# Attention and decode sampling in a decoder layer: an earlier place for the modulation pieces, far keys in their place, one load queue, and another order at the end of mixing

## The chip, the cores and the metric

The kernel runs on one core of a Trainium2 chip. A core has five engines, each with its own instruction stream: TensorE (PE in the profile, its weight loads PEld), VectorE (DVE), ScalarE (ACT), GpSimd (POOL) and SyncE (SP). They wait for one another through semaphores. Transfers are issued by an engine onto its queue (SPq, ACTq, POOLq) and are carried by DMA engines; the profile counts sixteen of them. The metric is the device time of one execution in microseconds; lower is better.

## The reference, cut to what matters

One step of one layer for a prompt of 1024 tokens and for eight decode sequences ("samples") of four new tokens each, with a cache of 2048 keys and values per sequence.

```
mod = silu(c) @ w_ada + b_ada;  sh1, sc1, gt1, sh2, sc2, gt2 = split(mod)
u = x * (1 + sc1) + sh1;  xa, ga, q, k, v = split(u @ w_in)
y_a = rglru_branch(xa, ga)                      # recurrent branch
y_b = merge over (window, dilation) in (128,1), (512,4), (2048,16) of softmax(q k^T / 8) v
      # sample: keys = cache of 2048 rows and the 4 new ones
mixed = concat(rms_norm(y_a), rms_norm(y_b)) @ w_out
x1 = layer_norm(alpha * x + gt1 * mixed);  u2 = x1 * (1 + sc2) + sh2
out = layer_norm(alpha * x1 + gt2 * hier_moe(u2))   # 4 groups x 4 experts, top 2
also returned: the caches with the new rows appended (k_win_sample, v_win_sample, ...)
```

A sample's query needs the last 512 rows of the cache (near) and, of the 1536 rows before, four of every sixteen (far).

## The kernel before

The program is a row of stages, each a block of five instruction streams that ends with a barrier: `front` (input projection, recurrent branch, part of the modulation), `attention` (prompt), `sampling` (the eight sequences), `mixing` (output projection, first layer norm, router logits), `routing`, `experts`, `finish`. Every order is written out by hand; nothing is scheduled by a planner.

**attention** goes through 32 steps, 4 pairs of heads times 8 query tiles of 128. Step `s` has `t = s % 8` and attends to `t + 1` key blocks, so a round of eight steps grows from short to long. In a step TensorE makes the scores of step `s + 2`, turns the probabilities of `s`, and multiplies the values of `s - 1`; VectorE masks and takes maxima, ScalarE makes exponentials. Beside this, `modulate(n)` (L1126 to L1132) computes one of 16 pieces of the modulation that the first stage left over: two groups (halves of the remaining columns) of eight row blocks, four matmuls of 512 columns each that add into one accumulator `psM`. It sits in odd steps: `if s % 2 == 1: modulate(s // 2)`. The weights of a piece (1 MiB) come through a ring of four, `a_wring`, which SP fills again once the piece four back is done (`s_mm`). VectorE adds the bias to a finished group at steps 15 and 31 and so frees the accumulator (`s_me`). After each fourth ring load SP issues a copy of one sequence's value cache, 4 MB from memory to memory (`out_v_s`); behind the ring it loads the near keys of the first four sequences into `ring0`, then the new rows. SP ends the stage with a wait for the copies.

**sampling** works on two groups of four sequences. Cached keys and values come as 32 pieces through ten slots: key pieces 0 to 15 (near and far of the first group, then of the second), value pieces 16 to 31 in the same order. A near piece is 512 rows (1 MiB); a far piece is 96 strips of four rows (0.75 MiB). Slots 0 to 3 are `ring0`, the others `ring1` (`s_ring` in the profile). SP loads near pieces (`near_load`), ScalarE far pieces (`far_load`, L1541 to L1545, at seven places of its stream). A load into a used slot waits for `consumed(n - 10)`, a count of transposes (`s_tp`) or of value units (`s_pv`). Sixteen units `u` turn the keys: 0 to 3 near and 4 to 7 far of the first group, 8 to 15 the second. `turn(u, h)` transposes, ScalarE and VectorE evict one half each, `scores(u)` multiplies. `squares` (L1491 to L1497) sums the squares of the attention output for its norm: ScalarE makes four chunks of 1024 columns, TensorE adds them, two token tiles in each of units 4 to 7. `values(g, part)` multiplies near (part 0) and far (part 1) values. At the end SP loads half of the output weights into the room of slots 2 and 3 (`wo_early`).

**mixing** takes eight token tiles of 128 and one tile of the 32 sample rows (`t = 8`): `product`, `residual`, `deviation`, `normalize`, `modulate` (giving `u2`), then router logits by way of `turn_u`, `turned_u`, `router`, `partial`, `gather`, `route`. POOL makes `x1` from the normalized tile, SP stores `x1` and then `u2` of a tile, and at the end waits until all have landed. The tail after the last product serves tiles 6, 7 and 8.

## Time and profile before

| | us |
|---|---|
| three runs | 1475.36, 1482.18, 1482.31 (median 1482.18) |
| profiled execution | 1476.67, its span 1474.9 |
| attention | 346.9 to 506.3 |
| sampling | 506.3 to 638.7 |
| mixing | 638.7 to 777.0 |
| routing, experts, finish | 777.0 to the end |

A stage begins in the table where SP issues its first load. Over the span TensorE is busy 1233.1 us (84%), VectorE 732.4 (50%), ScalarE 580.6 (39%), POOL 155.0 (11%); the mean granted clock of TensorE is 0.907. SP's queue (q1) carries 260 MB of the 316 MB, ScalarE's (q10) 32 MB. The shares are means over stages with different limits, so they are read stage by stage. In a timeline an instruction's line ends with the idle time of its engine just before it and what ended that. For a tile, the profile lists its transfers with the time from issue to landing (least, median, most).

### The profile page before, as it was taken

The page shows a single profiled execution, that of the slowest core. Times are in us where ns is not written, and L with a number is a line of the kernel's source. Part 1 is how long each engine was busy: PE and PEld are TensorE (multiplying, and loading weights), DVE is VectorE, ACT ScalarE, POOL GpSimd, SP SyncE. Part 2 cuts the span into 40 slices and gives each one's busy share as a digit, 9 for nine tenths or more (in the row PEclk, how much of TensorE's full clock was granted, in tenths as well). Part 3 has the DMA queues.
Part 4 walks back from the last instruction along what each step waited for, and adds up shares of the span by engine and source line. Part 5 has one row for each costly group of instructions (what it writes and reads, how often), then busy time and mean ns, then how long its engine had stood idle before and what let it go on. Part 6 is the DMA issues. An engine that isn't in the chain of part 4 may idle for free. (4 is left out here: it accounts for less than half of the span.)

```text
span 1474.9 us, 21260 instructions
## 1 busy us (share of the span) xinstructions
PE 1233.1 (84%) x7040; PEld 939.7 (64%) x7041; DVE 732.4 (50%) x1238; ACT 580.6 (39%) x849; POOL 155.0 (11%) x146
## 2 busy tenths in 40 slices
PE   5799899997999778589960389999999999989762
PEld 3799777783555567158740267777778878778520
DVE  3357515434666425255533365788531454673147
ACT  3554532102555413133320354677421453662123
POOL 0000000000000000004333300011000000000064
PEclk8899999997999968789975599999999999999976
DMA  9967811298866457964313385999541666573193
GB/s 337 353 237 273 292 68 60 95 338 300 307 235 237 132 158 235 277 207 149 118 60 124 133 292 203 364 365 362 209 179 57 228 228 227 206 263 115 50 379 130
DMA packets 103278, 316.42 MB, mean 215 GB/s; under 512 B 14157, under 2 KB 23037, under 8 KB 96538
## 3 DMA queue, kind: packets, MB, share of 16 engines
q1 hardware_dynamic: 83738, 260.30, 50.0%
q10 hardware_dynamic: 12464, 31.87, 6.7%
q0 software_dynamic: 7008, 23.34, 4.7%
q8 instruction: 42, 0.69, 0.2%
q14 instruction: 26, 0.21, 0.0%
HBM read 281.17 MB, written 101.43 MB: 259 GB/s over the span
## 5 line engine op out<-in xcount | busy, mean ns | idle before, releaser
L2597 PE MATMUL e_psY<-e_downh,e_hTh 128*128 128x512 f32 x224 | 96.2, 429 | 27.9 <-DVE e_hTl L2553 27.9
L2532 DVE TENSOR_TENSOR e_downl<-e_wd,e_downh 128x1024 fp32r<-128x1024 f32 x64 | 74.1, 1219 | 76.7 <-ACT e_downh L2432 76.7
L2599 PE MATMUL e_psY<-e_downl,e_hTh 128*128 128x512 f32 x224 | 91.1, 407 | 0.0
L2597 PE MATMUL e_psG<-e_gateh,e_xTh 128*128 128x512 f32 x224 | 90.8, 405 | 0.2
L2598 PE MATMUL e_psY<-e_downh,e_hTl 128*128 128x512 f32 x224 | 91.0, 406 | 0.0
L2597 PE MATMUL e_psG<-e_uph,e_xTh 128*128 128x512 f32 x224 | 90.8, 405 | 0.0
L2598 PE MATMUL e_psG<-e_gateh,e_xTl 128*128 128x512 f32 x224 | 90.5, 404 | 0.0
L2599 PE MATMUL e_psG<-e_gatel,e_xTh 128*128 128x512 f32 x224 | 90.2, 403 | 0.0
L2598 PE MATMUL e_psG<-e_uph,e_xTl 128*128 128x512 f32 x224 | 88.6, 395 | 0.0
L2599 PE MATMUL e_psG<-e_upl,e_xTh 128*128 128x512 f32 x224 | 88.6, 395 | 0.0
L546 PE MATMUL n_psA<-n_wh,u_h 128*128 128x512 f32 (+1 forms) x216 | 88.0, 407 | 0.4 <-DVE n_wl L805 0.4
L548 PE MATMUL n_psA<-n_wh,u_l 128*128 128x512 f32 (+1 forms) x216 | 85.9, 397 | 0.0
L547 PE MATMUL n_psA<-n_wl,u_h 128*128 128x512 f32 (+1 forms) x216 | 85.6, 396 | 0.0
L2437 ACT CAST e_xTh<-e_psT 128x512 fp32r<-128x512 f32 x56 | 32.7, 584 | 130.8 <-PE e_psT L2592 130.8
L2425 ACT CAST e_gateh<-e_wg 128x1024 fp32r<-128x1024 f32 x64 | 62.3, 1045 | 52.3 <-POOLq L2495 39.7
L2432 ACT CAST e_downh<-e_wd 128x1024 fp32r<-128x1024 f32 x64 | 62.4, 1046 | 49.9 <-DMA e_wd<-in_w_exp_down 25.0
L2526 DVE TENSOR_TENSOR e_gatel<-e_wg,e_gateh 128x1024 fp32r<-128x1024 f32 x64 | 74.1, 1220 | 13.0 <-ACT e_gateh L2425 12.9
L2526 DVE TENSOR_TENSOR e_upl<-e_wu,e_uph 128x1024 fp32r<-128x1024 f32 x64 | 74.0, 1217 | 3.6 <-ACT e_uph L2425 3.6
L2597 PEld LDWEIGHTS e_psY<-e_downh,e_hTh 128*128 128x128 f32 x224 | 43.7, 195 | 38.9 <-issue 30.7
L2425 ACT CAST e_uph<-e_wu 128x1024 fp32r<-128x1024 f32 x64 | 62.4, 1049 | 5.9 <-issue 4.5
L2537 DVE TENSOR_TENSOR e_xTl<-e_psT,e_xTh 128x512 fp32r<-128x512 f32 x56 | 38.5, 687 | 49.1 <-ACT e_xTh L2437 49.0
L2502 POOL COPY e_ids<-ids 128x1 int32 (+1 forms) x28 | 12.1, 431 | 436.3 <-PE e_psT L2592 436.3
(391 smaller groups left out, 2661.7 us busy)
## 6 DMA issues: line engine op xcount, KB each, us to landing
e_wg<-in_w_exp_gate SPq DMA_DIRECT2D x16, 2048.0 KB
e_wu<-in_w_exp_up SPq DMA_DIRECT2D x16, 2048.0 KB
e_wd<-in_w_exp_down SPq DMA_DIRECT2D x16, 2048.0 KB, 10.7
out_k_s<-in_cache_win_k SPq DMA_DIRECT2D x8, 4088.0 KB, 21.5
out_v_s<-in_cache_win_v SPq DMA_DIRECT2D x8, 4088.0 KB, 33.7
a_wring<-in_w_ada SPq DMA_DIRECT2D x16, 1024.0 KB, 7.7
scratch_y<-e_y ACTq DMA_DIRECT2D x56, 256.0 KB, 6.7
n_wr<-in_w_in SPq DMA_DIRECT2D x20, 512.0 KB, 7.4
```

Of the source, the lines that this page charges most:

```text
L546: nc.tensor.matmul(dst, lh, rh, start=(k == 0), stop=False)
L547: nc.tensor.matmul(dst, lh, rl, start=False, stop=False)
L548: last = nc.tensor.matmul(dst, ll, rh, start=False, stop=(k == KD - 1))
L2425: nc.scalar.copy(w[name][H_][:, k:k + 2, :], ew[name][:, k:k + 2, :]).then_inc(s_wh.sem, s_wh.unit)
L2432: nc.scalar.copy(w["down"][H_][:, k, :], ew["down"][:, k, :]).then_inc(s_dh.sem, s_dh.unit)
L2437: nc.scalar.copy(xT[H_][:, par, 4 * half:4 * half + 4, :], psT[:, :, :]).then_inc(s_xh.sem, s_xh.unit)
L2526: nc.vector.tensor_tensor(w[name][L_][:, 2 * i:2 * i + 2, :], ew[name][:, 2 * i:2 * i + 2, :], w[name][H_][:, 2 * i:2 * i + 2, :], ALU.sub ...
L2532: nc.vector.tensor_tensor(w["down"][L_][:, k, :], ew["down"][:, k, :], w["down"][H_][:, k, :], ALU.subtract).then_inc(s_dl.sem, s_dl.unit)
L2537: nc.vector.tensor_tensor(xT[L_][:, par, blocks, :], psT[:, :, :], xT[H_][:, par, blocks, :], ALU.subtract).then_inc(s_tc.sem, s_tc.unit)
L2597: nc.tensor.matmul(dst, left[H_], right[H_], start=first, stop=False)
L2598: nc.tensor.matmul(dst, left[L_], right[H_], start=False, stop=False)
L2599: return nc.tensor.matmul(dst, left[H_], right[L_], start=False, stop=last)
```

## The change

**Attention.** `modulate(s - 1)` stands in each of steps 1 to 16; VectorE adds the bias at steps 8 and 16. The ring of weights lies in the room of four further slots, `ring0["far"]`. SP issues the 16 ring loads without copies between, then the near keys of the first group, two copies, then (once all pieces are done) the first group's far keys into that room, two more copies, and the new rows.

In attention SP's stream holds, from the third weight load on, before (`a_wring` are weights, `out_v_s` a cache copy, `ring` near keys):
```order
L1060 DMA a_wring<-in_w_ada 128x2048 x2
L1067 DMA out_v_s<-in_cache_win_v 64x16352
L1060 DMA a_wring<-in_w_ada 128x2048 x4
L1067 DMA out_v_s<-in_cache_win_v 64x16352
L1060 DMA a_wring<-in_w_ada 128x2048 x4
L1067 DMA out_v_s<-in_cache_win_v 64x16352
L1060 DMA a_wring<-in_w_ada 128x2048 x4
L1067 DMA out_v_s<-in_cache_win_v 64x16352
L1070 DMA ring<-in_cache_win_k 128x2048 x4
L1072 DMA out_k_s<-scratch_k_new 8x2048
```
and of the change (`ring_far` are far keys):
```order
L1067 DMA a_wring<-in_w_ada 128x2048 x14
L1074 DMA ring<-in_cache_win_k 128x2048 x4
L1059 DMA out_v_s<-in_cache_win_v 64x16352 x2
L1080 DMA ring_far<-in_cache_win_k 96x2048 x4
L1059 DMA out_v_s<-in_cache_win_v 64x16352 x2
L1084 DMA out_k_s<-scratch_k_new 8x2048
```
The four copies moved behind the weights, and four loads of far keys came in among them.

**Sampling.** Slots 0 to 3 are `ring0`, 4 to 7 `ring_far`, and two are left in `ring1`. All remaining pieces, 8 to 31, are loaded by SP in the order of their numbers; ScalarE loads none. The squares' four chunks are added into one by VectorE (`add_squares`, units 2 to 4), and TensorE sums that one for all tiles in unit 6, eight matmuls. `scale` of the recurrent branch comes one unit later.

In sampling ScalarE's stream, which evicts the turned keys (`s_kTs`), held these rows before, from its start to the first load that it issues between evictions:
```order
L1545 DMA s_ring<-in_cache_win_k 96x2048 x4
L1549 COPY s_kown<-kT 128x128
L1531 COPY s_kTs<-s_psK 128x1024
L1556 ACTIVATE s_sqb<-ybT 128x1024
...
L1531 COPY s_kTs<-s_psK 128x8x96 x4
L1539 CAST yah<-gelu_in 128x1024
L1531 COPY s_kTs<-s_psK 128x1024
L1545 DMA ring<-in_cache_win_k 96x2048 x2
L1545 DMA s_ring<-in_cache_win_k 96x2048 x2
```
and SP's stream of the change, from the second group's keys to the output weights:
```order
L1384 DMA s_ring<-in_cache_win_k 128x2048 x2
L1384 DMA ring<-in_cache_win_k 128x2048 x2
L1386 DMA ring<-in_cache_win_k 96x2048 x2
L1386 DMA ring_far<-in_cache_win_k 96x2048 x2
L1384 DMA ring_far<-in_cache_win_v 128x2048 x2
L1394 DMA s_bias<-in_k_sbias 128x928
L1384 DMA s_ring<-in_cache_win_v 128x2048 x2
L1386 DMA ring<-in_cache_win_v 96x2048 x4
L1384 DMA ring_far<-in_cache_win_v 128x2048 x4
L1386 DMA s_ring<-in_cache_win_v 96x2048 x2
L1386 DMA ring<-in_cache_win_v 96x2048 x2
L1400 DMA wo_early<-in_w_out 128x1024 x4
```
The loads of far pieces (96 rows) left ScalarE's stream and stand in SP's, between the near ones (128 rows).

**Mixing.** SP stores `u2` of a tile before `x1`. At the end TensorE turns tile 7 before it gathers tile 6; ScalarE takes the partial sums of tile 6, the turned tile 7 and then the sample tile's deviation, with tile 7's partial sums before the normalization; VectorE takes the logits of tile 6 ahead of the sample tile's `u2`, and makes the sample tile's `x1`, which POOL made before. The wait for the stores stands in POOL's stream of `experts`, ahead of its first fetch; their semaphores live outside the stage.

On VectorE the last rows of mixing were, from the sample tile's residual (`x_z`) on:
```order
L1919 TENSOR_TENSOR x_z<-x_psA,xs_gt 32x1024
...
L1949 TENSOR_TENSOR logits<-x_psR,x_br 128x20
L1929 RECIPROCAL x_col<-x_col 32x1
L1932 TENSOR_TENSOR x_col<-x_col 32x1
L1941 TENSOR_TENSOR x_u_6288<-x_z,xs_sc 32x1024
L1942 TENSOR_TENSOR x_u_6288<-x_u_6288,xs_sh 32x1024
L1949 TENSOR_TENSOR logits<-x_psR,x_br 128x20 x2
L1949 TENSOR_TENSOR logits<-x_psR,x_br 32x20
```
and are now:
```order
L1931 TENSOR_TENSOR x_z<-x_psA,xs_gt 32x1024
...
L1941 RECIPROCAL x_col<-x_col 32x1
L1944 TENSOR_TENSOR x_col<-x_col 32x1
L1961 TENSOR_TENSOR logits<-x_psR,x_br 128x20
L1953 TENSOR_TENSOR x_u_6267<-x_z,xs_sc 32x1024
L1954 TENSOR_TENSOR x_u_6267<-x_u_6267,xs_sh 32x1024
L1990 TENSOR_TENSOR x_x_6273<-x_z,x_lng 32x1024
L1992 TENSOR_TENSOR x_x_6273<-x_x_6273,x_lnb 32x1024
L1961 TENSOR_TENSOR logits<-x_psR,x_br 128x20
L1961 TENSOR_TENSOR logits<-x_psR,x_br 32x20
```
One row of logits moved ahead of the sample tile's `u2`, and two operations for `x1` came in behind it.

The diff, without the lines that only hand on semaphores and buffers:

```diff
-                if n % 4 == 3:
-                    sp.dma_start(ov[b:b + 1, 0:PAST - TS, :], cv[b:b + 1, TS:PAST, :]).then_inc(s_cp.sem, s_cp.unit)
+            copy(CT)
+            copy(CT + 1)
+            sp.wait_ge(s_mm.sem, s_mm.at(PIECES))
+            for c in range(4):
+                sp.dma_start(ring0["far"][0:FARM, c, :, :], rows.rearrange("(m i) n -> m i n", i=16)[:, 0:4, :]).then_inc(s_ring0[4 + c].sem, s_ring0[4 + c].unit)
+            copy(CT + 2)
+            copy(CT + 3)
...
-                if s % 2 == 1:
-                    modulate(s // 2)
+                if 1 <= s <= PIECES:
+                    modulate(s - 1)
...
-                if s % 16 == 15:
-                    g = s // 16
+                if s in (KD, PIECES):
+                    g = s // KD - 1
...
+        early = (ring0["slots"], ring0["far"], ring1)
+        slot = lambda n: early[n % RING // 4][:, n % RING % 4, :, :]
...
+            def load(n):
                 if n >= RING:
                     s, value = consumed(n - RING)
                     sp.wait_ge(s.sem, s.at(value))
-                sp.dma_start(slot(n), rows_of(n)[PAST - NEAR:PAST, :].rearrange("(p i) n -> p i n", i=4)).then_inc(s_ring[n % RING].sem, s_ring[n % RING].unit)
-            for n in (*range(8, 12), *range(16, 20), *range(24, 28)):
-                if n == 10:
+                if n // 4 % 2 == 0:
+                    sp.dma_start(slot(n), rows_of(n)[PAST - NEAR:PAST, :].rearrange("(p i) n -> p i n", i=4)).then_inc(s_ring[n % RING].sem, s_ring[n % RING].unit)
+                else:
+                    sp.dma_start(slot(n)[0:FARM], rows_of(n)[0:PAST - NEAR, :].rearrange("(m i) n -> m i n", i=16)[:, 0:4, :]).then_inc(s_ring[n % RING].sem, s_ring[n % RING].unit)
+            for n in range(8, PIECES):
+                if n == 8:
...
+            def squares():
+                pe.wait_ge(s_sq2.sem, s_sq2.at(3))
-                for t in (t, t + 1):
-                    for c in range(CT):
-                        last = nc.tensor.matmul(psS[:, 1, SQ + t:SQ + t + 1], sq[:, c, t * P:(t + 1) * P], ones[:, 0:1], start=(c == 0), stop=(c == CT - 1))
+                for t in range(NT):
+                    last = nc.tensor.matmul(psS[:, 1, SQ + t:SQ + t + 1], sq[:, 0, t * P:(t + 1) * P], ones[:, 0:1], start=True, stop=True)
                 last.then_inc(s_sqs.sem, s_sqs.unit)
-                if 4 <= u < KT_:
-                    squares(2 * (u - 4))
+                if u == 6:
+                    squares()
...
-                if u == KT_:
-                    for n in range(12, 16):
-                        far_load(n)
-                if u < CT:
-                    nc.scalar.activation(sq[:, u, :], ybT[:, u, 0:SEQ], ACT.Square).then_inc(s_sq.sem, s_sq.unit)
+                if u < CT // 2:
+                    for c in (2 * u, 2 * u + 1):
+                        nc.scalar.activation(sq[:, c, :], ybT[:, c, 0:SEQ], ACT.Square).then_inc(s_sq.sem, s_sq.unit)
...
+            def add_squares(i):
+                if i < 2:
+                    v.wait_ge(s_sq.sem, s_sq.at(2 * i + 2))
+                    c, d = 2 * i, 2 * i + 1
+                else:
+                    v.wait_ge(s_sq2.sem, s_sq2.at(2))
+                    c, d = 0, 2
+                nc.vector.tensor_tensor(sq[:, c, :], sq[:, c, :], sq[:, d, :], ALU.add).then_inc(s_sq2.sem, s_sq2.unit)
-                if 4 <= u < 4 + CT:
-                    scale(0, u - 4, first)
+                if 2 <= u <= 4:
+                    add_squares(u - 2)
+                if 5 <= u < 5 + CT:
+                    scale(0, u - 5, first)
...
-                sp.wait_ge(s_x1.sem, s_x1.at(t + 1))
-                sp.dma_start(dram["x1"][t * P:t * P + n, :], x1[0:n, t % 2, :]).then_inc(s_o1[t % 2].sem, s_o1[t % 2].unit)
                 sp.wait_ge(s_u2.sem, s_u2.at(t + 1))
                 sp.dma_start(dram["u2"][t * P:t * P + n, :], u2[0:n, t % 2, :]).then_inc(s_o2[t % 2].sem, s_o2[t % 2].unit)
+                if t < NT:
+                    sp.wait_ge(s_x1.sem, s_x1.at(t + 1))
+                else:
+                    sp.wait_ge(s_x1q.sem, s_x1q.at(1))
+                sp.dma_start(dram["x1"][t * P:t * P + n, :], x1[0:n, t % 2, :]).then_inc(s_o1[t % 2].sem, s_o1[t % 2].unit)
...
-            for s in (s_o1, s_o2):
-                sp.wait_ge(s[0].sem, s[0].at(NT // 2 + 1))
-                sp.wait_ge(s[1].sem, s[1].at(NT // 2))
...
-            for t in range(NTT):
-                n, par = rows_of(t), t % 2
+            for t in range(NT):
+                n, par = P, t % 2
...
+                if t == NT:
+                    route(t - 2)
...
-            route(NT - 2)
+            v.wait_ge(s_o1[0].sem, s_o1[0].at(NT // 2))
+            nc.vector.tensor_tensor(x1[0:NS, 0, :], z[0:NS, 0, :], lng[0:NS, :], ALU.mult).then_inc(s_gq.sem, s_gq.unit)
+            v.wait_ge(s_gq.sem, s_gq.at(1))
+            nc.vector.tensor_tensor(x1[0:NS, 0, :], x1[0:NS, 0, :], lnb[0:NS, :], ALU.add).then_inc(s_x1q.sem, s_x1q.unit)
             route(NT - 1)
             route(NT)
...
                 if t == NT:
+                    partial(t - 2)
                     turned_u(t - 1)
                 deviation(t)
+                if t == NT:
+                    partial(t - 1)
...
-                if t >= 1:
+                if 1 <= t < NT - 1:
                     partial(t - 1)
...
+            turn_u(NT - 1)
             gather(NT - 2)
-            turn_u(NT - 1)
             router(NT - 1)
...
+            for rows in s_rows["x1"], s_rows["u2"]:
+                pool.wait_ge(rows[0].sem, rows[0].at(NT // 2 + 1))
+                pool.wait_ge(rows[1].sem, rows[1].at(NT // 2))
```

## Rows read from the trace of the kernel before

**Rows 1.** Stretches: length, busy (x) of PE, PEld, DVE, ACT, POOL, PEclk, DMA share, GB/s
```profile
356.00:501.00 145.00, 136.53 (x1198) 81.55 (x1190) 90.16 (x335) 76.98 (x196) 0.00 (x0) 0.99 0.68 251
...
538.00:562.00 24.00, 24.00 (x271) 22.26 (x270) 7.76 (x11) 5.40 (x6) 0.00 (x0) 0.59 0.33 114
595.00:615.00 20.00, 10.49 (x43) 1.96 (x44) 1.15 (x4) 4.46 (x5) 0.00 (x0) 0.66 1.02 281
```

**Rows 2.** Timeline of SP's queue: start, length, line, transfer, count
```profile
506.30 0.34 SPq L1363 DMA_DIRECT2D s_bias<-in_k_sbias  x1
...
517.33 0.81 SPq L1369 DMA_DIRECT2D ring<-in_cache_win_k  x2
...
638.74 1.75 SPq L1810 DMA_DIRECT2D x_wo_rest<-in_w_out  x4
```

**Rows 3.** Timeline of TensorE in sampling: start, length, line, tiles, [idle before <-releaser]
```profile
515.19 1.08 PE L1422 MATMUL s_psS<-s_kTs,s_qz 128*32 128x128 f32 x32
...
518.10 1.08 PE L1422 MATMUL s_psS<-s_kTs,s_qz 128*32 128x128 f32 x32
...
525.99 0.52 PE L1408 MATMUL s_psK<-ident,s_ring 96*128 96x96 f32 x4 [4.23 <-DMA s_ring<-in_cache_win_k]
...
556.73 1.95 PE L1408 MATMUL s_psK<-ident,s_ring 128*128 128x128 f32 x8
...
581.62 0.87 PE L1422 MATMUL s_psS<-s_kTs,s_qz 128*32 128x96 f32 x32
...
583.88 0.87 PE L1422 MATMUL s_psS<-s_kTs,s_qz 128*32 128x96 f32 x32
...
590.31 3.64 PE L1464 MATMUL s_psO<-s_ring,s_pT 128*32 128x512 f32 x32
```

**Rows 4.** Timeline of TensorE in attention's second round of eight steps
```profile
416.45 0.63 PE L1106 MATMUL a_psT<-ident,lg 128*128 128x128 f32 x4 [0.88 <-ACT pT L1239]
...
420.80 1.06 PE L1131 MATMUL a_psM<-a_wring,a_cT 128*32 128x512 f32 x8
```

**Rows 5.** Timeline of VectorE and POOL at mixing's end
```profile
747.95 0.16 DVE L1929 RECIPROCAL x_col<-x_col 128x1 f32<-128x1 f32 x1 [1.55 <-ACT x_col L1991]
...
764.24 0.15 DVE L1929 RECIPROCAL x_col<-x_col 32x1 f32<-32x1 f32 x1 [5.05 <-ACT x_col L1991]
...
767.13 1.21 DVE L1942 TENSOR_TENSOR x_u<-x_u,xs_sh 32x1024 f32<-32x1024 f32 x1
...
770.83 2.33 POOL L1855 TENSOR_TENSOR x_x<-x_x,x_lnb 32x1024 f32<-32x1024 f32 x1
```

**Rows 6.** The tile a_wring, whole run: from issue to landing
```profile
DMA to landing us min/median/max: 5.0/7.7/20.9
```

**Rows 7.** The tile ring, 460 to 462 us (issues that overlap it): durations, issue times, landing
```profile
L1070 SPq DMA_DIRECT2D ring<-in_cache_win_k x3: 486/523/609, 459.8 to 461.0; - x3
...
DMA to landing us min/median/max: 21.2/23.0/24.9
```

**Rows 8.** Groups by line, 380 to 640 us: count, busy us, mean ns, idle
```profile
L1496 PE MATMUL s_psS<-s_ones,s_sqb 128*128 128x1 f32 x64 | 12.7, 328 | 0.0
```

**Rows 9.** The tile s_ring, 551.5 to 554 us: near values on SP's queue
```profile
L1369 SPq DMA_DIRECT2D s_ring<-in_cache_win_v x2: 328/380/431, 552.0 to 552.3; - x2
...
DMA to landing us min/median/max: 4.7/5.8/6.8
```

**Rows 10.** The tile ring, 558 to 559.5 us: far keys on ScalarE's queue
```profile
L1545 ACTq DMA_DIRECT2D ring<-in_cache_win_k x2: 319/378/438, 558.7 to 559.1; - x2
...
DMA to landing us min/median/max: 5.5/6.9/8.3
```

**Rows 11.** The tile ring, 613 to 615 us: the last far values
```profile
L1545 ACTq DMA_DIRECT2D ring<-in_cache_win_v x2: 353/396/438, 614.0 to 614.4; - x2
...
DMA to landing us min/median/max: 11.0/13.1/15.1
```

**Rows 12.** Timeline of SP's queue: routing's first load
```profile
777.02 0.35 SPq L2181 DMA_DIRECT2D ranks<-in_k_ranks  x1
```

More of the change, by code:

```diff
@@ L142, in program @@
         silu = sb("silu", [P, KD, NSEQ])
-        s_ring0 = [Sem(nc.alloc_semaphore(f"ring{j}"), 16) for j in range(4)]
+        s_ring0 = [Sem(nc.alloc_semaphore(f"ring{j}"), 16) for j in range(8)]
         s_wo = [Sem(nc.alloc_semaphore(f"wo{j}"), 16) for j in range(4)]
+        s_rows = {n: [Sem(nc.alloc_semaphore(f"{n}_rows{p}"), 16) for p in range(2)] for n in ("x1", "u2")}
         s_cache = Sem(nc.alloc_semaphore("cache"), 16)
@@ L168, in program @@
                 sampling(nc, a, ident, qT, kT, v, gelu_in, ybT, ssq, at_v, split, ring0, s_ring0, s_wo)
-                mixing(nc, a, out, dram, ident, cols, gelu_in, ybT, ssq, logits, at_v, split, ring0, s_wo)
+                mixing(nc, a, out, dram, ident, cols, gelu_in, ybT, ssq, logits, at_v, split, ring0, s_wo, s_rows)
             with ExitStack() as c4:
@@ L192, in program @@
                     routing(nc, a, out, dram, ident, logits, route, ew)
-                    experts(nc, a, out, dram, ident, route, ew)
+                    experts(nc, a, out, dram, ident, route, ew, s_rows)
                 finish(nc, a, out, dram, ident, route, s_cache, 12)
@@ L1053, in _, with copy @@
             b_ada = a["b_ada"].rearrange("(o n) -> o n", o=1)
+            def copy(b):
+                sp.dma_start(ov[b:b + 1, 0:PAST - TS, :], cv[b:b + 1, TS:PAST, :]).then_inc(s_cp.sem, s_cp.unit)
             sp.wait_ge(s_mz.sem, s_mz.at(1))
@@ L1307, in sampling @@
         s_b = S("s_b", 16)
-        s_ring = [*s_ring0, *(S(f"s_r{j}", 16) for j in range(4, RING))]
+        s_ring = [*s_ring0, *(S(f"s_r{j}", 16) for j in range(8, RING))]
         s_z = S("s_z")
@@ L1539, in upper @@
                 nc.scalar.copy(dst[:, c, 0:SEQ], src[:, c, 0:SEQ]).then_inc(s_hi.sem, s_hi.unit)
-            def far_load(n):
-                if n >= RING:
-                    s, value = consumed(n - RING)
-                    act.wait_ge(s.sem, s.at(value))
-                nc.scalar.dma_start(slot(n)[0:FARM], rows_of(n)[0:PAST - NEAR, :].rearrange("(m i) n -> m i n", i=16)[:, 0:4, :]).then_inc(s_ring[n % RING].sem, s_ring[n % RING].unit)
-            for n in range(4, 8):
-                far_load(n)
             nc.scalar.copy(kown[:, :, :], kT[:, :, SEQ:TOK]).then_inc(s_own.sem, s_own.unit)
@@ L1564, in _ @@
                     nc.scalar.copy(pT[0:FARM, 4:8, :], psP[0:FARM, :, :]).then_inc(s_pc.sem, s_pc.unit)
-            for n in range(20, 24):
-                far_load(n)
             act.wait_ge(s_lg.sem, s_lg.at(2))
@@ L1570, in _ @@
             nc.scalar.copy(weights[1][0:FARM, 4:8, :], turn_to[1][1][0:FARM, :, :]).then_inc(s_pc.sem, s_pc.unit)
-            for n in range(28, 30):
-                far_load(n)
             for c in range(CT):
                 upper(1, c)
-            for n in range(30, 32):
-                far_load(n)
         @block.vector
@@ L1692, in _, with mixing @@
             add(1)
-def mixing(nc, a, out, dram, ident, cols, ya, ybT, ssq, logits, at_v, split, ring0, s_wo):
+def mixing(nc, a, out, dram, ident, cols, ya, ybT, ssq, logits, at_v, split, ring0, s_wo, s_rows):
     GA = 32
@@ L1778, in mixing @@
         s_lo = S("x_lo")
-        s_o1 = [S(f"x_o1{p}", 16) for p in range(2)]
-        s_o2 = [S(f"x_o2{p}", 16) for p in range(2)]
+        s_o1, s_o2 = s_rows["x1"], s_rows["u2"]
         block = ctx.enter_context(nc.Block())
@@ L2303, in _, with experts @@
             st.link(nc.vector.tensor_copy(route["ids"][:, :], psI[:, :]))
-def experts(nc, a, out, dram, ident, route, ew):
+def experts(nc, a, out, dram, ident, route, ew, s_rows):
     with ExitStack() as ctx:
```

30 lines of the change are left out of this document (15 added, 15 removed).

## The prediction

> **What bounds the kernel now.** The table of stages comes first: the change touches attention, sampling, mixing and one wait of the experts, so only the stretch from 346.9 to 777.0 us counts. The stretches of the span come second [rows 1]. In attention TensorE is busy 136.5 of 145 us; DMA moves 251 GB/s beside it. In sampling the columns turn round: from 595 to 615 us TensorE works 10.5 of 20 us at a granted clock of 0.66 while the DMA share is 1.02 at 281 GB/s, and from 538 to 562 us TensorE is full at 0.59, near its lower level of 1.2 GHz, while DMA is at 0.33. So sampling, 132.4 us long [rows 2], waits for loads at its two ends and leaves DMA idle between. TensorE's timeline names the loads: far keys of the first group (4.23 us here, and a second wait of 4.33 us right after) [rows 3].
>
> **Names.** A piece is one sequence's keys or values of one kind: near (512 rows, 1 MiB) or far (96 strips of 4 rows, 0.75 MiB). Pieces 0 to 3 are near keys of the first group, 4 to 7 its far keys, 8 to 15 the same for the second group, 16 to 31 the values in that order. Units 0 to 15 turn the keys; ten slots hold pieces.
>
> **Attention.** A modulation piece is four matmuls, 1.06 us [rows 4]. Eight of the sixteen stay on odd steps 1 to 15; eight move from steps 17 to 31 to the even steps 2 to 16. On TensorE that is +8.5 us early and -8.5 us late. Neither is whole: an even step has waits that the piece fills (0.88 us for a copy [rows 4], four such waits of 1.7 us together in a round of eight steps), and the same waits open in late odd steps that lose a piece. One new wait: piece 8 now follows piece 7 by one step instead of two, and it needs VectorE's sum of the accumulator, queued there behind a write; I take 0.7 us on TensorE (512 columns, half of a 1.21 us operation of 1024 [rows 5]), 0 and 2 as its ends. Sum +1, bounds -3 and +4. The weight ring still lands in time: pieces landed 5.0 to 20.9 us after issue [rows 6], the long ones behind a cache copy, which now comes later; with four in flight and a step of about 4.9 us (145 / 32 is 4.5 with half a piece, and half a piece less a wait is added) the ring covers 19 us.
>
> Behind the last ring piece (freed in step 12: the first piece ran at 356, 12 x 4.9 later it is 415 us) SP now puts 4.2 MB of near keys, two copies (8.4 MB), 3.1 MB of far keys and two copies. One copy with four near pieces, 8.4 MB from 458.6 us, had landed at 485.9 (461.0 + 24.9) [rows 7], 311 GB/s; 24.1 MB and a ring piece still in flight take 81 us, to about 496, plus 2 for the rows that follow. The next stage began only at 506.3 [rows 2]: 8 us of cover. The far keys land near 470, 50 us before unit 4 reads them.
>
> **Sampling, TensorE's side.** Units 0 to 3 stay as they are; unit 4 starts near 521, 5 us ahead of its first wait [rows 3]. Units 4 to 7 have their keys: where nothing waited, a far unit took 2.26 us (581.62 to 583.88 [rows 3]), four take 9. The squares shrink from 64 matmuls (12.7 us) [rows 8] to 8, with three sums on VectorE (1.2 us each, as 1024 columns take [rows 5]) beside TensorE's 2.9 us a near unit (515.19 to 518.10 [rows 3]); I allow 1.5 us. So unit 8 starts near 531 instead of 556.7 [rows 3]; with four near and three far units (11.6 and 6.8) and 3.5 us for the turned probabilities unit 15 turns near 553, and the first four value units (3.64 us [rows 3]) end at 563. Without VectorE's cover the three sums cost 3.7 us, which the DMA below hides.
>
> **Sampling, the DMA side, which I expect to end last.** Two near pieces alone on SP landed at 556.7 and 559.1 [rows 9]: 2.4 us each and 2.3 of latency. Two far pieces on ScalarE's queue landed at 564.2 and 567.4 [rows 10]: 3.2 us. Bounds for a far piece: 2.1 (3.2 less the 464 KB mask that ran in between, at the near rate), and 4.1, from the mixed stretch at 281 GB/s [rows 1]: two near and two far, 3.67 MB, take 13.1 us, less 4.8. I take 3.2, the row of the far pieces themselves.
> - Pieces 8 and 9 go out at once, 10 to 13 when unit 3 has turned, 517.3 as now [rows 2]: landed 517.3 + 2.3 + 4.8 + 6.4 = 530.8.
> - 14 to 17 are freed by unit 7 (about 530): 532.3 + 11.2 = 543.5.
> - 18 to 21 by unit 11 (542): 544.3 + 11.2 = 555.5.
> - 22 to 25 by unit 15 (553): 555.5 + 11.2 = 566.7.
> - 26 to 29 by the values at 563: 577.9. 30 and 31, freed at about 568: 584.3.
>
> In the profile the last far piece landed at 629.5 (614.4 + 15.1) [rows 11] and the stage ended 9.2 us later, at 638.7 [rows 2]. So the new end is 593.5: -45 us. With far pieces at 2.1 the releases decide, the last landing is 578.5: -51; at 4.1 all queue up behind each other, last landing 593: -36. ScalarE loses the issues of all sixteen far pieces and their waits; behind them stood only its own evictions and casts, which nothing here was late for, so 0. SP takes them over; behind a waiting load on SP stand only later loads and the output weights, which need be there only at 593.5 and land by about 590.
>
> On the number of queues the rows say that two near pieces on one queue move at 437 GB/s (1.05 MB in 2.4 us [rows 9]), while both queues together move 281 [rows 1]. The Trainium skill, "DMA: Bandwidth & Descriptors", section "Issuing engines are not separate DMA queues", says that queues share the same 16 engines and that spreading saves only issue time; by it one queue is no faster than two, and the mixed rate should stay, which is the second case below.
>
> **The mixing tail.** Before, the sample tile's deviation waits on ScalarE behind an eviction that waits for a late transpose: VectorE idles 5.05 us where the tile before had 1.55 [rows 5], so 3.5 us go. The u2 rows, done at 768.3 (767.13 + 1.21 [rows 5]), are then done at 764.8. The last x1 tile was two POOL operations of 2.33 us, ended at 773.2 [rows 5]; it becomes two VectorE operations of 1.21 us: 767.4. The two last logits follow at 768.3. The final wait for both stores to land moves to POOL in the experts, where they have long landed. Routing's first load came at 777.0 [rows 12], 3.9 us after that x1, for a store, its landing and the change of stage. I give the change alone 1.2 us (0 to 3.9 are its ends): 769.5. That is -7.5; bounds -4 and -9. Storing u2 ahead of x1 in the loop: 0, since TensorE is the bound there and the rows wait for it.
>
> **Sum.** +1 - 45 - 7.5 = -51.5 from the profiled 1476.7 us: 1425. The profiled execution stands 5.5 us below the median of the three runs and 2.4 below the mean of all four; a new measurement can fall on either, so 1428.
>
> **Rivals.**
> 1. The mixed rate is the rate, one queue or two. From 517.3 ten near and twelve far pieces and a mask, 20.4 MB, at 265 GB/s (just below the mixed row) take 77 us; with 2.3 latency the last lands near 597, the stage ends at 606: -32.5 instead of -45, so 1440; at 250 GB/s, 1445. For it: the mixed stretch was long and full. Against: the near pair alone. The rule cited above would give this case.
> 2. The late copies hold attention up. SP's stream ends with them, and the stage change waits. At 250 GB/s, the mean of the stage [rows 1], 25.2 MB from 415 end at 516 and 2 more for the rows: +12, 1440. Against: the 311 GB/s of the pair above [rows 7].
> 3. The gain is given back: sampling ends early but experts' weight loads or the clock absorb it, 1474 to 1482. Against: nothing past 777 depends on a clock time, only on routing's order.
> 4. Slower: the ring of weights starves. A piece is now due in each of steps 1 to 16 instead of every second; four in flight give one per quarter of the landing time. Above 4 x 4.9 = 19.6 us a step waits, and above 33 us 16 waits of 3.3 us eat all 52. The worst landing was 20.9, behind a copy [rows 6], and no copy stands there now. At 36 us it would be 16 x 4.1 = 66, so 1494.
> That the far keys aren't there at unit 4 is no real case: 50 us of cover.
>
> **How the numbers follow.** Forecast 0.62, its own range 1416 to 1440 (the far bounds, -51 and -36, and half of the tail's and attention's). Rival 1 0.20, rival 2 0.10, rival 3 0.04, rival 4 0.04. The range 1414 to 1446 holds the forecast and most of rivals 1 and 2, leaving out about 0.15. A measurement of this kernel can tell 0.5%, 7.4 us, from no change: the forecast and rivals 1 and 2 are faster, 0.92; rival 3 is the same, 0.04; rival 4 slower, 0.04.
>
> **What would show it.** Attention ends within 4 us of 501, with no weight-ring wait over 1 us on TensorE and the DMA still idle in its last microseconds. Units 4 to 7 show no DMA wait, and unit 8 starts between 528 and 536. In sampling's second half TensorE waits for value pieces, and the landing of far pieces behind each other tells 3.2 us from 2.1 or 4.1. The stage takes 80 to 97 us. From the last sample-tile product to routing's first load there are about 13 us instead of 20.7. It is wrong if sampling still takes over 110 us, if attention grows by more than 5 us, or if stages after routing change length.

## The result, and the profile after

The changed kernel takes 1439.36 us (median of four runs, 1437.60 to 1443.61) against 1478.99 for the kernel before in the same session (four runs, 1475.36 to 1482.31): ratio 0.9737, 95% interval 0.9699 to 0.9775. The forecast was 1428 with a range of 1414 to 1446. The profiled execution took 1438.72 us (span 1436.9, mean granted clock 0.917).

By stage, from SP's first loads [rows 2, 12 for before]:

| | before | after | difference | forecast |
|---|---|---|---|---|
| attention | 159.4 | 159.5 | 0 | +1 |
| sampling | 132.4 | 99.6 | -32.9 | -45 |
| mixing | 138.3 | 130.9 | -7.3 | -7.5 |
| routing to the end | 697.9 | 700.1 | +2.2 | 0 |

These are SP's issues after (start, length, line, transfer, count); they answer to [rows 2, 12]:
```profile
506.27 0.35 SPq L1377 DMA_DIRECT2D s_bias<-in_k_sbias  x1
...
517.87 1.09 SPq L1386 DMA_DIRECT2D ring<-in_cache_win_k  x2
...
545.33 0.81 SPq L1384 DMA_DIRECT2D s_ring<-in_cache_win_v  x2
...
574.69 0.78 SPq L1386 DMA_DIRECT2D ring<-in_cache_win_v  x2
575.51 1.91 SPq L1400 DMA_DIRECT2D wo_early<-in_w_out  x4
...
605.84 2.95 SPq L1825 DMA_DIRECT2D x_wo_rest<-in_w_out  x4
...
736.78 0.35 SPq L2201 DMA_DIRECT2D ranks<-in_k_ranks  x1
```
The stretches answer to [rows 1] (length, busy of PE, PEld, DVE, ACT, POOL, granted clock, DMA share, GB/s):
```profile
356.00:501.00 145.00, 136.44 (x1198) 81.57 (x1198) 89.86 (x335) 77.26 (x196) 0.00 (x0) 0.99 0.78 270
538.00:562.00 24.00, 18.91 (x396) 16.38 (x395) 15.99 (x18) 10.27 (x14) 1.63 (x1) 0.96 0.94 298
575.00:595.00 20.00, 12.38 (x58) 3.06 (x54) 5.65 (x7) 0.35 (x1) 0.00 (x0) 0.82 1.02 258
```
Attention does the same TensorE work in the same 145 us and DMA carries more beside it. The hole in the middle of sampling is filled: the DMA share from 538 to 562 us was 0.33 and is 0.94. But the full stretch at the end moves only 258 GB/s, less than the 281 of before, with one queue now. TensorE's timeline (answers to [rows 3]):
```profile
520.60 1.49 PE L1425 MATMUL s_psK<-ident,ring_far 96*128 96x96 f32 x16
...
533.21 1.09 PE L1425 MATMUL s_psK<-ident,s_ring 128*128 128x128 f32 x8
...
561.81 3.75 PE L1505 MATMUL s_psK<-s_dg,s_ones 128*128 128x512 f32 x4 [3.40 <-issue]
...
581.74 6.53 PE L1481 MATMUL s_psS<-ring_far,s_kTs 128*32 128x512 f32 x26 [3.64 <-DMA ring_far<-in_cache_win_v]
...
594.82 1.06 PE L1481 MATMUL s_psS<-ring,s_kTs 96*32 96x512 f32 x1 [2.46 <-DMA ring<-in_cache_win_v]
```
Unit 4 starts at 520.6 with no wait for its key (4.23 us before), unit 8 at 533.2, and the waits left are for value pieces: 3.64 us at 581.7, 2.46 us for the last one, which landed at 594.7.

The weight ring [rows 6], the two near value pieces issued at 545.3, and the last two far ones (answers to [rows 11]), from issue to landing:
```profile
DMA to landing us min/median/max: 4.9/6.5/9.1
```
```profile
L1384 SPq DMA_DIRECT2D s_ring<-in_cache_win_v x2: 328/380/433, 545.3 to 545.7; - x2
...
DMA to landing us min/median/max: 10.0/10.0/10.0
```
```profile
L1386 SPq DMA_DIRECT2D ring<-in_cache_win_v x2: 313/370/427, 574.7 to 575.0; - x2
...
DMA to landing us min/median/max: 16.6/18.2/19.7
```
VectorE at mixing's end (answers to [rows 5]):
```profile
728.60 0.15 DVE L1941 RECIPROCAL x_col<-x_col 32x1 f32<-32x1 f32 x1 [1.55 <-ACT x_col L2008]
...
733.87 1.21 DVE L1992 TENSOR_TENSOR x_x<-x_x,x_lnb 32x1024 f32<-32x1024 f32 x1
...
735.62 0.17 DVE L1961 TENSOR_TENSOR logits<-x_psR,x_br 32x20 f32<-32x20 f32 x1 [0.45 <-PE x_psR L2111]
```
The 5.05 us wait is 1.55, as in the tiles ahead of it, and the last `x1` is done at 735.1.

So two terms came as forecast and sampling gave 12 us less. After the fact, those 12 us are: 3.3 because unit 11 released its slots at 545.3 and not at 542, so that loading resumed at 547.6 instead of 544.3; 7.1 because the six near and eight far pieces from there to the last landing took 47.1 us instead of 40.0; 1.9 because the end behind the landing took 11.1 us instead of 9.2 (the granted clock was 0.66 there, and 1.00 in the 9.2 us of before). Of the 3.3 us, 2.2 had come up before unit 8 started (533.2 instead of 531): from 529 to 535 us TensorE was busy throughout at a granted clock of 0.72. The experiments ask about the 7.1, and then price each part of the change.

### The profile page after: what moved, and what is told of

Read it like the earlier page. It is cut to its first block and busy times, and to the rows that moved or that the text cites. A ratio compares the mean times of both kernels' runs of the same rounds, so it can differ in the third digit from the quotient of the medians.

```text
span 1436.9 us, 21162 instructions
## 1 busy us (share of the span) xinstructions
PE 1214.6 (85%) x6992; PEld 922.1 (64%) x6993; DVE 740.2 (52%) x1243; ACT 582.1 (41%) x849; POOL 148.6 (10%) x144
## 5 line engine op out<-in xcount | busy, mean ns | idle before, releaser
L2457 ACT CAST e_xTh<-e_psT 128x512 fp32r<-128x512 f32 x56 | 32.9, 587 | 127.2 <-PE e_psT L2615 127.1
L2452 ACT CAST e_downh<-e_wd 128x1024 fp32r<-128x1024 f32 x64 | 62.5, 1048 | 51.9 <-DMA e_wd<-in_w_exp_down 28.9
## 6 DMA issues: line engine op xcount, KB each, us to landing
out_k_s<-in_cache_win_k SPq DMA_DIRECT2D x8, 4088.0 KB, 20.8
```

The costliest lines, as they stand in the source:

```text
L2452: nc.scalar.copy(w["down"][H_][:, k, :], ew["down"][:, k, :]).then_inc(s_dh.sem, s_dh.unit)
L2457: nc.scalar.copy(xT[H_][:, par, 4 * half:4 * half + 4, :], psT[:, :, :]).then_inc(s_xh.sem, s_xh.unit)
```

## The experiments

Kernels of one session share the runs of the kernel before. A ratio is to the kernel before; a stage's length is from one profiled execution. The part from routing to the end is the same work in every kernel and took 695.8 to 704.0 us in them, so single executions can differ by some 8 us there, and 2.2 means nothing. Sampling itself took 132.4, 135.7 and 135.1 us in the three kernels that leave it as it was before, so a difference of some 3 us between two executions of that stage means little.

### Loads measured by themselves, first set

```
for c in range(8): sp.dma_start(tile["far"][0:96, c], strips(c, 16)[:, 0:4])   # then a wait; nine such groups
```


> The changed kernel with a stage ahead of it that only loads cached keys into free memory, in nine groups, each begun when the one before has landed: eight near pieces (1 MiB, 128 strips of 8 KiB that lie one behind the other); eight far pieces (0.75 MiB, 96 strips of 8 KiB, one every 32 KiB); 96 strips without gaps; one strip every 40 KiB; every 16 KiB; far pieces as four loads of 2 KiB rows; far pieces with the strips dealt in another order; near and far in turn on one queue; four near on SP beside four far on ScalarE's queue. Theory A, the address pattern makes a far piece dear: near 2.4 us a piece (19 us for eight, and 2 of latency), far 4.1 (33), without gaps 1.8 (14.4, as 0.75 of near), every 40 KiB between these; near and far in turn 26 for eight, two queues the same 26. Theory B, a far piece is dear only beside near pieces or other loads: far alone 1.8 to 3.2 us a piece (14 to 26 for eight) like the strips without gaps, and only the last two groups at 26. If 32 KiB as a power of two is what costs, 40 KiB is as fast as no gaps.

SP's timeline; a group starts when the one ahead of it has landed:
```profile
0.76 4.13 SPq L218 DMA_DIRECT2D p_near<-in_cache_win_k  x8
22.93 4.04 SPq L221 DMA_DIRECT2D p_far<-in_cache_win_k  x8
50.55 3.84 SPq L224 DMA_DIRECT2D p_cont<-in_cache_win_k  x8
78.61 3.92 SPq L227 DMA_DIRECT2D p_pitch<-in_cache_win_k  x8
105.97 3.99 SPq L230 DMA_DIRECT2D p_pitch<-in_cache_win_k  x8
132.03 15.27 SPq L234 DMA_DIRECT2D p_single<-in_cache_win_k  x32
159.05 5.78 SPq L238 DMA_DIRECT2D p_turned<-in_cache_win_k  x8
188.20 0.37 SPq L242 DMA_DIRECT2D p_alternate<-in_cache_win_k  x1
...
214.51 1.85 SPq L248 DMA_DIRECT2D p_two<-in_cache_win_k  x4
```
and the rate inside the first three groups (columns as above):
```profile
3.00:20.00 17.00, 0.00 (x0) 0.00 (x0) 0.00 (x0) 0.00 (x0) 0.00 (x0) 1.00 1.01 425
25.00:48.00 23.00, 0.00 (x0) 0.00 (x0) 0.00 (x0) 0.00 (x0) 0.00 (x0) 1.00 1.02 250
53.00:76.00 23.00, 0.00 (x0) 0.00 (x0) 0.00 (x0) 0.00 (x0) 0.00 (x0) 1.00 1.03 244
```
Start to start, eight near pieces take 22.2 us, eight far ones 27.6 with three quarters of the bytes. Less 2.2 us of latency that is 2.5 and 3.2 us a piece: my forecast's far piece was right for far pieces by themselves. Theory A falls: strips without gaps take 28.1 us, one every 40 KiB 27.4, every 16 KiB 26.1, as 2 KiB rows 27.0, in another order 29.2. The addresses matter little, and not in the theory's direction. Theory B falls too: a far piece is dear without any near one beside it, and near and far in turn take 26.3 us, little more than their own prices (4 x 2.5 + 4 x 3.2 + 2.2 = 25.0). What all the far forms share is that they land on 96 partitions.

### Far pieces from neighbouring rows, in the kernel

```
-rows_of(n)[0:PAST - NEAR, :].rearrange("(m i) n -> m i n", i=16)[:, 0:4, :]
+rows_of(n)[0:4 * FARM, :].rearrange("(m i) n -> m i n", i=4)
```


> The changed kernel, but each far piece of sampling from piece 12 on reads 384 rows that lie one behind the other instead of 96 strips of 4 rows 32 KiB apart: the same bytes, partitions, queue and order (so other keys and values are used than the reference's). Theory A (address pattern): a far piece takes about 1.8 us instead of 4.1, the releases decide, sampling ends near 590 instead of 605.8, the kernel at about 1424. Theory B (the shared engines or the total rate, whatever the addresses): sampling's loads stay at 4.1 us a far piece and the kernel at 1439. Theory C (the early output weights and late releases): sampling also stays within 3 us.

Ratio 0.9725 (0.9681 to 0.9768), sampling 96.9 us. The same loads without gaps are no better than 2.7 us, within what single executions differ by: theory A falls in the kernel too.

### Output weights later

```
-s, value = consumed(v_piece(0, 1, 3)); sp.wait_ge(s.sem, s.at(value))
+sp.wait_ge(s_ring[31 % RING].sem, s_ring[31 % RING].at(31 // RING + 1))
```


> The changed kernel with the four early output-weight loads (2 MiB) issued only when the last value piece has landed, instead of right behind it in the queue. Theory C (these loads take engine time from the last value pieces): the last piece lands 3 to 5 us earlier, near 591, and sampling ends near 602; kernel 1435, if the weights, landing near 599, don't hold up mixing. Theories A and B: in-order engines gain nothing from it, the last piece stays at 594.7 within 1 us, and the kernel within 2 us of 1439 or up to 5 later if mixing waits for the weights.

Ratio 0.9674 (0.9631 to 0.9717), overlapping the changed kernel's; sampling 102.4 us in the profiled execution (1446.3 us, above the median of 1437.3). There piece 18 was issued at 549.8 and the last landed at 579.3 + 20.2 = 599.5, 49.7 us later; after, it was 545.3 to 594.7, 49.4. Theory C falls: the weights took nothing from the value pieces. Its stretches near the end:
```profile
586.00:594.00 8.00, 7.10 (x35) 2.38 (x36) 0.05 (x1) 0.00 (x0) 0.00 (x0) 0.64 1.03 202
594.00:597.00 3.00, 1.94 (x4) 0.14 (x2) 2.58 (x4) 0.00 (x0) 0.00 (x0) 1.00 0.60 134
```
With nothing queued behind, the DMA share is 0.60 in the last three microseconds before the last piece can be used: some of the sixteen engines seem to be done while others are not. The profile does not list them one by one.

### Far pieces back on ScalarE's queue

```
+if u == KT_:            # ScalarE, behind its eviction of unit 8
+    for n in range(12, 16): far_load(n)     # 20 to 23, 28 to 31 at their old places
```


> The changed kernel with the far pieces from 12 on put back on ScalarE's queue, at the places in ScalarE's program that they had before; the attention part, the ten slots and the rest stay. By my forecast's step (far pieces leave ScalarE's program, one queue is a gain in itself) sampling grows by 5 to 12 us, to a kernel of 1445 to 1450. By the Trainium skill, page DMA: Bandwidth & Descriptors, section Issuing engines are not separate DMA queues, the queue alone changes nothing while the engines are full: sampling within 3 us of 99.6, kernel 1437 to 1442.

Ratio 0.9838 (0.9796 to 0.9879), sampling 118.3 us: 18.7 longer, more than either theory said. ScalarE's issues and TensorE's waits tell why (two views):
```profile
531.41 1.15 ACTq L1560 DMA_DIRECT2D ring<-in_cache_win_k  x2
```
```profile
549.58 0.90 PE L1425 MATMUL s_psK<-ident,ring 96*128 96x96 f32 x4 [4.23 <-DMA ring<-in_cache_win_k]
554.70 0.87 PE L1425 MATMUL s_psK<-ident,ring_far 96*128 96x96 f32 x4 [4.21 <-DMA ring_far<-in_cache_win_k]
559.56 0.90 PE L1425 MATMUL s_psK<-ident,ring_far 96*128 96x96 f32 x4 [3.99 <-DMA ring_far<-in_cache_win_k]
```
Pieces 12 and 13 could go out when unit 3 had turned, and do so on SP at 517.9 after; on ScalarE their place is behind the eviction of unit 8, at 531.4. The whole stage, here and then after (columns as above):
```profile
504.04:622.38 118.34, 86.43 (x1034) 55.65 (x1034) 49.86 (x71) 29.66 (x35) 4.45 (x5) 0.80 0.75 216
```
```profile
506.30:605.80 99.50, 84.22 (x1034) 53.11 (x1034) 49.85 (x71) 29.47 (x35) 4.43 (x5) 0.86 0.85 256
```
The bytes are the same, some 25.5 MB. DMA idles for about 30 us here (0.25 of 118.3) and 15 after, so about 15 of the 18.7 us are DMA time without work: the place in an instruction stream. The other 4 are a lower rate while DMA is busy. Whether two queues cause that is not shown, since no run moves the queue and leaves the places. The Trainium skill, DMA: Bandwidth & Descriptors, section Issuing engines are not separate DMA queues, says that DMAs run on the same 16 engines whichever engine issues them, and that issuing from several saves only the time of issuing. The first set of loads agrees in that a second queue gained nothing: four near and four far pieces took 26.3 us in turn on one queue (316 GB/s from 191 to 212 us) and 28.9, the end of that stage included, on two (274 GB/s from 217 to 240 us).

### Far pieces on 128 partitions, more bytes

```
-slot(n)[0:FARM] <- rows_of(n)[0:PAST - NEAR, :] ... "(m i) n -> m i n", i=16 ... [:, 0:4, :]   # 96 strips
+slot(n)         <- rows_of(n)                   ... "(m i) n -> m i n", i=16 ... [:, 0:4, :]   # 128 strips
```


> The changed kernel with each far piece loaded as 128 strips instead of 96: the 32 more strips lie in the near rows, land on the partitions 96 to 127 and are never read. 1 MiB instead of 0.75 MiB a piece. Theory A2, from the separate loads (96 partitions took 3.2 us a piece with and without gaps, 128 took 2.5): a load is dear because it has 96 partitions, so more bytes come sooner; twelve pieces in sampling at 0.7 us less are -8, sampling 91 to 93 us, kernel 1431. Rival, bytes at one mixed rate of 281 GB/s: 3.1 MB more are +11 us, kernel 1450.

Median 1429.00, ratio 0.9647 (0.9610 to 0.9683), sampling 89.1 us: 10.4 less, with 3.1 MB more to load. One stretch of it:
```profile
557.00:587.00 30.00, 24.34 (x235) 8.12 (x229) 13.35 (x21) 5.55 (x8) 0.00 (x0) 0.92 1.00 398
```
Near and far together move at 398 GB/s on one queue; of a near and a far piece together an eighth is never read. Theory A2 holds and the mixed rate as a limit of its own falls.

### Far rows as 128 partitions times three

```
-KT_ = 8; near = [P] * 4 + [FARM] * 4
+KT_ = 7; near = [P] * KT_
+for j in range(3):
+    sp.dma_start(slot(n)[:, j, :], rows_of(n)[512 * j:512 * (j + 1), :].rearrange("(m i) n -> m i n", i=16)[:, 0:4, :])
...
+far = 16 * (np.arange(TS * FARM) // TS) + np.arange(TS * FARM) % TS     # order of the mask's columns
```


> The changed kernel with the 384 far rows of a sequence laid on 128 partitions times three rows instead of 96 times four: three loads of 128 rows of 2 KiB each, three units of 128 keys instead of four of 96, three blocks of turned weights. Same bytes, 128 partitions. Theory A2: a far piece takes 0.75 of a near one, 1.85 us, twelve in sampling at 1.35 us less than the 3.2 measured alone are -16; then the releases by TensorE decide more often, so sampling 85 to 90 us and the kernel 1425 to 1430. Rival: 384 rows of 2 KiB cost more than 96 strips of 8 KiB, or SP needs 1.3 us to issue three loads and becomes the bound: sampling 95 to 100 us, kernel 1435 to 1440.

Median 1423.67, ratio 0.9611 (0.9585 to 0.9637), sampling 80.5 us, below what I expected, and the best version here by its median: 19 us shorter than the changed kernel's stage. Its interval overlaps that of the wide far pieces, so that it beats those is not shown. A stretch of its loads:
```profile
555.00:577.00 22.00, 18.45 (x121) 5.34 (x120) 11.86 (x20) 5.42 (x7) 0.00 (x0) 1.00 1.00 382
```
Rows of 2 KiB are no dearer than strips of 8 KiB. Fewer units spare TensorE work besides, and its granted clock is 1.00 in this stretch, where it was 0.82 in the last 20 us of loads after; how the 19 us divide among the three is not shown.

### The kernel before with wide far pieces

```
-nc.scalar.dma_start(slot(n)[0:FARM], rows_of(n)[0:PAST - NEAR, :] ...)
+nc.scalar.dma_start(slot(n), rows_of(n) ...)
```


> The kernel before, two queues and all, with each far piece loaded as 128 strips instead of 96 (the 32 more are never read). If the 96 partitions set the mixed rate of 281 GB/s, the stretches with near and far loads together rise to about 410 GB/s, twelve or more far pieces come 0.7 us sooner each and the waits at both ends shrink: sampling 118 to 124 us instead of 132.4, kernel 1468. If two queues in turn have a rate of their own near 281, 3.1 MB more make sampling about 140 us, kernel 1490.

Ratio 0.9867 (0.9811 to 0.9923), sampling 120.7 us. From 595 to 615 us it moves 344 GB/s at a share of 0.86, where before moved 281 at 1.02 [rows 1]:
```profile
595.00:615.00 20.00, 15.55 (x82) 3.68 (x80) 5.65 (x7) 0.00 (x0) 0.00 (x0) 0.73 0.86 344
```
The low mixed rate of before, on which rival 1 rested, was that of the 96 partitions, with two queues as with one.

### The mixing tail alone

The mixing functions and the experts' waits of the change in the kernel before, nothing else.

> The kernel before with the mixing part of the change alone: the sample tile's deviation and logits order, its last x1 operations on VectorE, u2 stored ahead of x1, and the final wait for the stores moved to POOL in the experts. My step: mixing 138.3 -> 130.8 us (-7.5, bounds -4 and -9), kernel 1471.5. Rival: what the tail gives is taken back by routing and the experts: mixing shorter, kernel within 2 us of before.

Ratio 0.9948 (0.9926 to 0.9969), about -7.7 us; mixing 130.2 us, -8.1. My step holds by itself and nothing behind takes it back.

### The attention order alone

```
-if s % 2 == 1: modulate(s // 2)
+if 1 <= s <= PIECES: modulate(s - 1)          # VectorE's two sums at steps 8 and 16
```


> The kernel before with the attention order alone: a modulation piece in each of the steps 1 to 16; the cache copies stay between the loads of the weight ring and the far keys stay on ScalarE's queue in sampling. My step for TensorE alone is +1 us (-3 to +4). My fourth rival's mechanism should show here, since the copies were not moved away: per four pieces 4 MiB of weights (10 us) and one copy (4.2 MB, 13.5 us at 311 GB/s) are 23.5 us against 4 x 4.9 = 19.6 us of steps, so TensorE waits about 4 us a round of four, 8 to 16 us in all, kernel 1487 to 1495. If the copies don't hold the ring up: 1478 to 1481.

Ratio 1.0064 (1.0039 to 1.0089): slower. From the first ring load to sampling it takes 165.8 us instead of 158.4. The tile `a_wring` in this kernel (idle of TensorE's matmuls and weight loads by cause: us, times; then issue to landing):
```profile
  DMA a_wring<-in_w_ada: 17.1, 6
...
DMA to landing us min/median/max: 6.8/20.1/22.3
```
A ring piece lands 20.1 us after issue in the median (7.7 before [rows 6], 6.5 after), and TensorE's matmuls or weight loads idle six times for one (17.1 us in all; 2.9 in two places before). Rival 4's mechanism is real; the change escapes it because it takes the copies out of the ring's way.

### The squares as 64 matmuls

```
-if u == 6: squares()
+if 4 <= u < KT_: squares(2 * (u - 4))         # add_squares on VectorE left out
```


> The changed kernel with the sum of squares as it was: 64 matmuls in four parts behind units 4 to 7 instead of three sums on VectorE and 8 matmuls. My step counted 12.7 us of TensorE less 1.5, hidden behind the loads where DMA ends last. If DMA covers it: unit 8 starts 9 to 11 us later (542 instead of 533.2), but 14 to 17 are then released later by the same time and the chain of loads, busy from 547 on, can hide only its idle share of about 4 us: sampling 104 to 108 us, kernel 1445. If all is hidden: sampling within 2 us of 99.6, kernel 1439.

Ratio 0.9761 (0.9713 to 0.9810), sampling 108.0 us, +8.4. The profile lists each of these matmuls twice, so the 64 are 32 in the program, and the 8 of the change are 16 in the profile: 11.2 us of TensorE here, 1.9 after, where the forecast allowed 1.5. The granted clock falls to 0.50 among the 64. In this stretch of the run DMA has next to nothing to load:
```profile
536.00:548.00 12.00, 12.00 (x93) 11.28 (x97) 2.21 (x4) 2.14 (x3) 0.00 (x0) 0.50 0.07 14
```
Unit 8 starts 38.7 us after the stage's first load (26.9 after), unit 11 frees its slots 11.0 us later, and the loads behind win back only some 2 of these. So the loads hide little of the squares: they wait for the slots that TensorE frees. In the ratio the two kernels can't be told apart.

### The first group's far keys loaded in sampling

```
-for c in range(4): sp.dma_start(ring0["far"][0:FARM, c], ...)     # attention
-for n in range(8, PIECES): ...
+for n in range(4, PIECES): ...                                    # sampling
```


> The changed kernel without the load of the first group's far keys in attention: SP loads them as the first thing of sampling, on the same queue, ahead of pieces 8 and 9. The price of the early load: four far pieces of 3.2 us, 12.8 us of DMA, against about 4 us of idle DMA between 517 and 547 us and some before 517; unit 4 waits about 3 us for its key and later loads follow 8 to 10 us later: sampling 107 to 110 us, kernel 1447 to 1450. If the early load is worth nothing (hidden): 1439.

Ratio 0.9757 (0.9711 to 0.9802), sampling 104.4 us, +4.8, below the 7 to 10 expected. The first unit of these keys waits 1.00 us only; of the 12.8 us of loads some 8 go into DMA time that was idle between the loads, most of it before 547 us: the DMA share of the stage is 0.93, against 0.85 after.

### Loads measured by themselves, second set

```
for c in range(8): sp.dma_start(tile["hundred_twelve"][0:112, c], near(c)[0:112])   # and so on, nine groups
```


> The changed kernel with a second stage of loads ahead of it, eight pieces a group, each group begun when the one before has landed: strips of 8 KiB onto 112, 80, 64 and 32 partitions (contiguous rows); far strips onto the partitions 32 to 127; far strips as two loads, 64 and 32 partitions; far rows as three loads of 128 rows of 2 KiB; four near pieces and then four far ones in one go; far strips of the values. Known: 128 partitions 2.5 us a piece (425 GB/s), 96 partitions 3.2 (250). If any count but 128 drops the rate to about 250 GB/s: 112 partitions take 3.7 us (30 for eight and 2 of latency), 80 take 2.6 (21). By the Trainium skill, page SBUF, section on the DMA port swizzle, the time goes by the port that gets most partitions: 64 partitions reach 8 of 16 ports and take 2.5 us a piece, as 128 do, 32 take 1.25, 112 and 80 take 2.5; by that rule 96 would have taken 2.5 too, not 3.2, so it can't be all. Three loads of 128 rows: 1.85 us (15 to 17 for eight). Four near and four far in a row: 22.8 and 2 of latency if nothing is lost between them, 26 or more if the far ones hold the near ones up. Values like keys, 27.6.

SP's timeline, as in the first set:
```profile
0.75 3.89 SPq L217 DMA_DIRECT2D p_hundred_twelve<-in_cache_win_k  x8
30.55 3.85 SPq L220 DMA_DIRECT2D p_eighty<-in_cache_win_k  x8
54.16 5.04 SPq L223 DMA_DIRECT2D p_sixtyfour<-in_cache_win_k  x8
77.35 3.57 SPq L226 DMA_DIRECT2D p_thirtytwo<-in_cache_win_k  x8
89.45 3.86 SPq L229 DMA_DIRECT2D p_upper<-in_cache_win_k  x8
115.04 0.47 SPq L232 DMA_DIRECT2D p_halves<-in_cache_win_k  x1
...
145.55 15.86 SPq L237 DMA_DIRECT2D p_three<-in_cache_win_k  x24
166.37 2.09 SPq L240 DMA_DIRECT2D p_row<-in_cache_win_k  x4
...
191.05 3.95 SPq L245 DMA_DIRECT2D p_values<-in_cache_win_v  x8
```
Less 2.2 us, a piece of 112 partitions takes 3.45 us, of 80 2.7, of 64 2.6, of 32 1.2; far strips on partitions 32 to 127 take 2.9, as 64 and 32 partitions 3.5. Only 128 partitions go beyond 275 GB/s. The Trainium skill, SBUF — State Buffer, section Door 1: The DMA port swizzle, says that bandwidth goes by how many of 16 ports the partitions reach, and that 64 reach only eight. That agrees with 64 partitions taking as long as 128, and 32 half of it; by an estimate from its table of ports, with the fullest port setting the time, 96, 112 and 80 partitions would take 2.5 us too, and the runs show 3.2, 3.45 and 2.7, so the measurement decides. Three loads of 128 rows took 20.8 us for eight pieces, more than the 15 to 17 expected. SP issued for 15.9 us of it, but the DMA share was 1.00 at 353 GB/s from 150 to 164 us, so the engines were full meanwhile. Four near and four far in a row took 24.7, about 4 x 2.5 + 4 x 3.2 + 2: nothing is lost between them.

## Why the prediction was right, and where it was off

The time came out inside the range, but not by the forecast's own sum: sampling gained 32.9 us, less than the 36 to 51 that I had as its bounds, and took 99.6 us, outside the 80 to 97 that I had named. The range held because its upper end made room for rivals 1 and 2. That the result fell on rival 1's number is in part luck.

- **Attention, +1: 0.** The ring was late only for its first piece (0.9 us, 0.7 before), and pieces landed after 9.1 us at most against 20.9 before; the wait for VectorE's sum was 0.3 us, where I took 0.7. The attention order alone shows that the copies' new place was needed for that. DMA was done some 10 us before the stage ended, as argued, so rival 2 fell.
- **Sampling, TensorE's side.** Unit 4 without a wait, unit 8 at 533.2 (forecast 531, named window 528 to 536), unit 15 at 554.6 (553). A new idle time of 3.4 us ahead of the second broadcast was not in the sum; it seems to have cost nothing, since DMA stayed full beside it (share 1.00 to 1.04 from 555 to 564 us) and the value loads end last.
- **Sampling, the DMA side: the step that was mis-sized.** "I take 3.2, the row of the far pieces themselves" was right for far pieces alone (3.2), but inside this stage a far piece cost (47.1 - 6 x 2.5) / 8 = 4.0 us, close to the upper bound of 4.1 that I had kept. The DMA share over these 47.1 us was 1.01, so they were work and not waiting. The releases were 3.3 us late, and the end 1.9 us longer. The number of rival 1 came out (stage end 606 forecast, 605.84 measured), and its 265 GB/s was near as a mean of this mixture (12.6 MB of pieces in 47.1 us are 267). Its mechanism, a rate that any mixture has, did not hold: the versions on 128 partitions move 398 and 382 GB/s on one queue, 344 at a DMA share of 0.86 on two. The 96 partitions do it.
- **What stays open:** of the 0.8 us between 3.2 alone and 4.0 in the stage, 0.2 is the lower rate there (234 GB/s from 582 to 593 against 250). The rest, some 5 us over eight pieces, goes where pieces land later than the mean rate says: the near pair with far pieces behind it landed 10.0 us after issue, the pair of before with nothing behind 4.7 and 6.8 [rows 9]. The packets say that the DMA engines finish apart. From 589 to 594 us, the last 5 us before the last far piece landed, 27 packets are of 8 KiB, the far pieces' size, and 216 are the 4 KiB ones of the weights behind them (253 under 8 KB, less 37 under 2 KB). So some engines were done with the value pieces some 5 us before others. Why they drift apart here is open: by themselves, four near and four far pieces in a row left DMA full to the end (share 1.01 from 178 to 190 us, the next group begun at 191.05). The value 234, and the packets:
```profile
582.00:593.00 11.00, 9.30 (x40) 2.40 (x32) 2.63 (x4) 0.00 (x0) 0.00 (x0) 0.74 1.02 234
```
```profile
DMA packets 280, 1.11 MB, mean 221 GB/s; under 512 B 37, under 2 KB 37, under 8 KB 253
```
- **The queue.** I let ScalarE's loss of the issues count 0 and put the gain into the chain of releases; the run with the far pieces back on ScalarE prices that at 18.7 us of the stage, more than half of its gain, about 15 of it as idle DMA. The squares (8.4) and the early keys (4.8, little above what single executions differ by) follow, each undone alone; the parts overlap and do not add up exactly.
- **The mixing tail, -7.5: -7.3**, and -8.1 alone; from the end of the last product to routing's first load it took 12.5 us (about 13 forecast).
- **Rival 3** (given back) fell: +2.2 us after routing is within what executions differ by there.

## What to carry to other kernels

Price a load by the partitions that it lands on, before its bytes: on this chip a load of 128 partitions that fetches a third more came sooner than one of 96, and a layout that fills 128 partitions without them took another 8.6 us off the stage (one execution each, and with fewer units for TensorE). A load belongs into the instruction stream in which its buffer's release is the next thing waited for; on another engine it waits for that engine's work. A rate read from a stretch with several kinds of loads belongs to that mixture: measure each kind alone before saying what sets it.
